# Identity matmuls issued on TensorE at the begin of the expert stage and ahead of the final sums

## The reference

```python
def expert_step(acc, args):
    wg, wu, wd, cw = args
    hh = jax.nn.silu(x @ wg) * (x @ wu)
    return acc + (hh * cw[:, None].astype(hh.dtype)) @ wd, None
y, _ = lax.scan(expert_step, jnp.zeros_like(x), (w_gate, w_up, w_down, combine.T))
...
xp = xp + g2 * hier_moe(...)
y_prompt = rmsnorm(xp, norm_final)
```

## Time and profile before

| | us |
|---|---|
| median of three executions | 1245.49 |
| lowest and highest | 1238.99, 1247.1 |
| the profiled execution, its time | 1240.19 |
| its span, from first to last record | 1238.4 |
| TensorE busy | 1100.7 (89% of the span) |
| VectorE, ScalarE, GpSimd busy | 491.6, 356.3, 366.4 |
| chain that ended last: PE, DMA, DVE | 17%, 9%, 3% of the span (the shares listed do not add up to the whole) |
| TensorE clock granted, mean over the span | 0.955 of full |

### The profile page before, as it was taken

One profiled execution on the slowest core, in us unless ns is written; L12 is line 12 of the kernel. 1 busy time (PEld: TensorE's weight loads), 2 busy tenths in 40 slices (PEclk: granted clock), 3 DMA queues, 4 the chain that ended last, 5 costly groups with the idle time before them and its releaser, 6 DMA issues. The chain is left out here.

```text
span 1238.4 us, 20082 instructions
## 1 busy us (share of the span) xinstructions
PE 1100.7 (89%) x7180; PEld 767.1 (62%) x7180; DVE 491.6 (40%) x1307; ACT 356.3 (29%) x1130; POOL 366.4 (30%) x306
## 2 busy tenths in 40 slices
PE   5589999999999899999986899962999999989956
PEld 2348788888888788888875688851333333333322
DVE  0453344444444344453555267754111212111227
ACT  2643334434334334433454122210111111011102
POOL 1150633535353403113033144435222222121001
PEclk8799999999999999999999899975999999999978
DMA  9953323223141504021077511125999999999784
GB/s 382 404 196 110 96 69 108 93 64 101 62 118 34 166 1 120 14 72 45 1 221 212 188 69 69 69 103 215 398 374 373 413 414 393 406 368 422 281 306 158
DMA packets 86809, 238.63 MB, mean 193 GB/s; under 512 B 10456, under 2 KB 58024, under 8 KB 75952
## 3 DMA queue, kind: packets, MB, share of 16 engines
q1 hardware_dynamic: 68384, 132.01, 30.5%
q10 hardware_dynamic: 7344, 78.91, 15.8%
q0 software_dynamic: 10976, 26.32, 5.7%
HBM read 208.19 MB, written 38.45 MB: 199 GB/s over the span
## 5 line engine op out<-in xcount | busy, mean ns | idle before, releaser
L1987 PE MATMUL moe_gu_ps<-a_gu,moe_xT_sb 128*64 x416 | 185.1, 598 | 5.2 <-DMA b_gu<-in_w_gu 3.3
L942 PE MATMUL att_piece_ps<-hT_hi,w_hi 128*128 128x384 f32 (+1 forms) x528 | 184.4, 349 | 2.4 <-PEq L196 1.0
L1990 PE MATMUL moe_gu_ps<-b_gu,moe_xT_sb 128*64 128x512 f32 x416 | 185.1, 598 | 0.0
L942 PE MATMUL att_piece_ps<-hT_hi,w_lo 128*128 128x384 f32 (+1 forms) x528 | 172.7, 327 | 0.0
L942 PE MATMUL att_piece_ps<-hT_lo,w_hi 128*128 128x384 f32 (+1 forms) x528 | 172.5, 327 | 0.0
L1167 DVE COPY att_pT_sb<-att_pT_ps 128x512 f32<-128x512 f32 (+2 forms) x192 | 94.6, 520 | 133.4 <-PE att_pT_ps L1010 132.9
L1987 PEld LDWEIGHTS moe_gu_ps<-a_gu,moe_xT_sb 128*64 128x64 f32 x416 | 57.0, 138 | 125.7 <-issue 125.7
L1271 ACT ACTIVATE att_probs_sb<-att_probs_sb,att_nmax_sb 128x640 f32<-128x640 f32 (+5 forms) x144 | 101.4, 704 | 41.3 <-DVE att_nmax_sb L1153 40.6
L1289 ACT ACTIVATE keep_rows_all_sb<-att_o_ps,att_rden_sb 128x64 f32<-128x64 f32 x144 | 37.3, 310 | 246.8 <-PE att_o_ps L1031 246.8
L942 PEld LDWEIGHTS att_piece_ps<-hT_hi,w_hi 128*128 128x128 f32 x528 | 99.1, 188 | 11.1 <-issue 6.0
L1153 DVE CUSTOM_DVE_ANT_0 att_probs_sb<-att_s_ps,both_wide_sb 128x640 f32<-128x640 f32 (+5 forms) x144 | 95.3, 662 | 26.8 <-PE att_s_ps L998 15.0
(11 more groups left out here) (312 smaller groups left out, 1964.1 us busy)
## 6 DMA issues: line engine op xcount, KB each, us to landing
b_gu<-in_w_gu ACTq DMA_DIRECT2D x25, 2048.0 KB
b_dn<-in_w_dn ACTq DMA_DIRECT2D x25, 1024.0 KB
a_gu<-in_w_gu SPq DMA_DIRECT2D x10, 2048.0 KB
keep_rows_all_sb<-in_w_ada SPq DMA_DIRECT2D x9, 2048.0 KB, 11.2
att_w_raw_sb<-in_w_qkv SPq DMA_DIRECT2D x21, 512.0 KB, 3.7
a_dn<-in_w_dn SPq DMA_DIRECT2D x10, 1024.0 KB
w_out_parts<-keep_rows_all_sb SPq DMA_DIRECT2D x16, 512.0 KB, 4.8
in_w_ada_sb<-in_w_ada SPq DMA_DIRECT2D x3, 2048.0 KB, 16.6
```

What stands on the lines that cost most here:

```text
L942: ins = pe.matmul(bank[:, 0:hi - lo], w[:, kind, kc, :], x[:, kc, lo:hi], start=(m == 0), stop=(m == 3 * NC - 1))
L1987: pe.matmul(gu_ps[p % 2][LANE[0], :], xT[:, c, LANE[0]], a_gu[:, bass.ds(slot, 1), c, :].rearrange("p a n -> p (a n)"), start=(c == 0), st ...
L1990: ins = pe.matmul(gu_ps[p % 2][LANE[1], :], xT[:, c, LANE[1]], b_gu[p % 3][:, c, :], start=(c == 0), stop=(c == NC - 1))
```

## The change

A function `run_up(m)` issues m products of the identity with the first 512 columns of `rows_all` into the first bank of `gu_all_ps`, without any wait and without signalling anybody. It is called three times on TensorE: with 3 before the wait for the columns of the table, with 2 between the products of the table and the first `transpose_x`, and with 12 between the rounds and the loop of the final sums. The results are never read: the next product that uses the bank overwrites it. No other engine's instructions change.

```diff
+        def run_up(m):
+
+            for _ in range(m):
+                pe.matmul(gu_all_ps[:, 0, :], ident, rows_all[:, 0, 0:512], start=True, stop=True)
+
+        run_up(3)
         pe.wait_ge(cols_done, 1)
         for m in range(4):
             pe.matmul(y_ps[0:1, m * LOOK:(m + 1) * LOOK], cols[:, m:m + 1], ident[:, 0:LOOK], start=True, stop=True)
         pe.matmul(y_ps[0:1, 4 * LOOK:4 * LOOK + 1], cols[:, 4:5], ident[:, 0:1], start=True, stop=True)\
           .then_inc(table_ready, 1)
+        run_up(2)
         transpose_x(0)
         pe.wait_ge(table_set, 1)
         gate_up(0)
...
         in_rounds(pe, look(pe, T_ROUNDS, 0, 1, ROUNDS), body)
+        run_up(12)
 
         for t in range(TILES):
             r = rows_of(t)
```

## The result

The changed kernel takes 1254.51 us, the median of 7 executions (1252.19 to 1260.69), against 1241.63 (1238.99 to 1247.54) of the kernel before, 7 executions too. The ratio is 1.0097 with a 95% interval of 1.0071 to 1.0123: slower by 12 us, 9 to 15. (By the two medians alone it is 12.9.) The forecast was 1253.5, and +10.3 us for the change; 10.3 of 1241.63 is 0.83%, inside the interval.

A forecast was written before the change was run, and what follows sets the result against it. TensorE's sequencer, held in four jumps until 1191.95, was taken to bound the end. Twelve products +10.3 us, the rest 0: +10.3, giving 1253.2 on the mean and 1255.8 on the median; predicted 1253.5, range 1246 to 1260.

The forecast's parts named there:

- The place of the twelve products: Ahead of the final sums: they stand behind TensorE's four jumps, so start at 1191.95, on the path; net +10.3 us.
- The cheap bound of +8.0: Final sums: if the sequencer comes through by 1189.66, when the data lands, 2.3 us of the twelve are covered.
- Their price: Twelve products ahead of the sums: first sum 13.10 us after their start, tile 0 gives back 2.79; net +10.3 us.
- the larger chance: Whole kernel: chance of 0.81 that the time stays within 1%, 12.5 us, of the kernel before.
- The cover of the five products: Begin of the expert stage: waits hide three products with 2.7 us left and two with 1.1; cost 0.
- The clock at the begin: Transposes and gate_up: whether the five products raise their clock; -3.0 us at most, 0 taken as likelier.
- The bound of 3.0 us: Begin: most the raised clock could give, up to 0.9 us in the transposes and 2.1 in gate_up.
- The hole as a real one: Rival (5%), ahead of the final sums: branches take little, the twelve fill the idle time; -5.1 us, with the begin -8.1.
- The further stall: Rival (10%), behind the branches: sequencer waits again for code, 3.0 to 5.9 us more; +13.3 to +16.2.
- The short branch time: TensorE's branches: the skill's about 0.108 us each, 0.43 for four, would make the real hole the forecast; trace has 2.98 to 5.86.

The follow-up runs named there:

- begin_only: The changed kernel without the twelve products, so only the three and two at the begin, against the kernel before: 1242.66 us, ratio 0.9994.
- begin_longer: The kernel before with six products ahead of the table and five behind it, none ahead of the final sums: 1241.91 us, ratio 0.9998.
- between_jumps: The kernel before with its four jumps kept and 3, 4 and 6 products between them, none behind the last: 1240.68 us, ratio 0.9975.
- begin_longer_one_jump_end: The kernel before with six and five products at the begin, nested rounds with one far jump, twelve products ahead of the sums: 1238.25 us, ratio 0.997.
- all_three_again: Repetition, against the kernel before: six and five products at the begin, one far jump, twelve products ahead of the sums; 1239.25 us, ratio 0.9972.

## Why the prediction was right

**The place of the twelve products.** It rested on reading the 13.43 us of "issue" as four jumps. In the trace after, the jumps stand as before and the products start at the end of the last. The experiment that has one jump moves them into the hole and turns their sign: against the same kernel without them they give -1.3 us in the traces in place of +10.5, and jump and products together -5.1. The sentence that no instruction behind the branches can use the hole was too strong: it holds in five of the seven traces with four jumps, and in the other two the jumps end some 4.5 us before the data lands. The cheap bound of +8.0 counted 2.3 us of cover.

**Their price.** 13.10 us less 2.79 was worked out; the trace has 12.75 and 6.23 - 3.43 = 2.80, so 9.95, and 10.1 to the end of the span. Twelve alone were +8.3 by the times, six alone +4.8; 0.859 us each lies inside both intervals. That the forecast time of 1253.5 came within 1.0 us of the measured 1254.51 is partly luck: the sum was put on some 1243.2, while the median before is 1241.63 with more executions, and 10.3 on that gives 1251.9. It was also close that the change stayed within 1%, as the larger chance had it: the ratio is 1.0097. The 12 us between the changed kernel and the one before is 2 more than the sum. The interval covers it, and the products at the begin do not explain it, since alone they measured -0.7 us with an interval of 3 to each side.

**The cover of the five products.** It held, with 3.40 us to spare in place of 2.7 and 1.09 as forecast at 1.1. The first figure differs because the clock rose during the three: they took 4.55 us, not 5.3.

**The clock at the begin.** Its worth was taken as 0 with the better chance, and so it was: the clock was raised by the three and lost in the wait. In the trace of begin_only it was lost in the next wait instead. The bound of 3.0 us was right too: in begin_longer the transposes took 0.87 us less than before, and the starts of gate_up's first and last slot lay 6.5 us apart (863.60 to 870.10) in place of 8.6, together 2.9. What the prediction did not name is the wait that ends last then, the gather of the second step's rows. It looked for the loss some 170 us later, in the weights and the scatters; there was some there also, but in begin_longer the first 3.10 us went at the very next gather. In the two traces with all three parts that wait was 1.4 us and none.

**The rivals.** The hole as a real one was worked out at -5.1 us, if TensorE came by 1179.4; the kernels with one jump fulfil that condition, and gave it. The further stall did not appear: the twelve products are gapless. The short branch time is contradicted in each trace: the jumps over unused rounds took 1.6 to 6.6 us, all but two of them about 3 or more, and the one far jump out of the nest 3.5 to 4.5.

## What to carry to other kernels

Idle time of an engine's array is not time in which its program can do more: read what the sequencer does in it, above all behind branches, before anything is put there. Work that only fills must stand between the jumps that make the hole, or the jumps must go first; here one far jump in place of four was worth 2 to 3 us, and the filler behind it then stopped costing 10. Where filler makes an engine early, look up the next transfer it waits for: the gain can end there.

## What the runs showed of the hardware

- The last jump of TensorE's sequencer took 5.8 to 6.6 us in the traces in which it began after SP's loads of rows, and 3.3 and 3.4 us in between_jumps and begin_longer, where it began 0.6 and 0.7 us ahead of them. In the changed kernel's trace VectorE, ScalarE and GpSimd jumped over their own unused rounds in at most 0.06 us each.
- In the trace before, the DMA queue named "instruction" moved one packet of 16 KB in each of the four long jumps: two in the window 1176:1180, one in 1180:1184, and, in the jump that began at 1186.1, none in 1186:1188, where the loads of rows kept the DMA engines 97.5% busy, and one in 1188:1190. That a jump ends only when its packet is there, and is long because the packet stands behind the loads, fits these rows; no run tests it.
- TensorE's array goes on with what was issued while its sequencer is in a jump: 13 products fill 11.63 us of jumps without a gap that the view shows.
- The clock that three products had raised was lost in the wait of 3.4 us behind them in one trace; in another, where that wait was 2.5 us, it was up behind it, and went in the next, of 2.7 us. With waits of 0.3 us at both places it stayed up.
- The barrier ahead of the expert stage was passed between 845.0 and 855.3 us in the thirteen traces, with the same instructions ahead of it; in two executions of one and the same kernel (begin_longer_one_jump_end and all_three_again) at 845.8 and 853.0. In the two traces compared in windows, the later one had the lower clock there. How much of the spread between executions comes from this was not measured.
